# Key pages of mixer A and of its index: turned on the host and loaded page by page from SyncE, instead of gathered by GpSimd and turned on TensorE

## The reference

```python
ki_all = concatenate([cache_a_kidx[page_table].reshape(n, PAST_LEN, D_IDX), ki], axis=1)
sc = where(causal, index_scores(qi, wi, ki_all), -inf)        # sum_h w * relu(q_idx . k_idx)
_, idx = lax.top_k(sc, 256)
k_g, v_g = cache_a_k[phys, off], cache_a_v[phys, off]         # or the new rows
out_a = attend_selected(qa, k_g, v_g, idx <= qpos)            # softmax(q k / 8) v
```

## Time and profile before

| | us |
|---|---|
| median of 3 runs (2168.15 to 2175.05) | 2169.51 |
| the profiled execution, its own time | 2170.43 |
| its span | 2168.6 |
| first part, before the first gather (0 to 444.2) | 444.2 |
| the stretch of `idx` (735.6 to 905.6) | 170.0 |
| the stretch of `sel` up to `a0` (1451.8 to 1501.3) | 49.5 |
| `a0` to `a7` (1501.3 to 1877.7) | 376.4 |

### The profile page before, as it was taken

One profiled execution on the slowest core, in us unless ns is written; L12 is line 12 of the kernel. 1 busy time (PEld: TensorE's weight loads), 2 busy tenths in 40 slices (PEclk: granted clock), 3 DMA queues, 4 the chain that ended last, 5 costly groups with the idle time before them and its releaser, 6 DMA issues.

```text
span 2168.6 us, 27262 instructions
## 1 busy us (share of the span) xinstructions
PE 1698.0 (78%) x8774; PEld 1236.0 (57%) x8774; DVE 1602.5 (74%) x3603; ACT 1257.1 (58%) x2751; POOL 635.5 (29%) x657
## 2 busy tenths in 40 slices
PE   7997699776896985996977987975887796765766
PEld 3554565635664654674655765654655665564554
DVE  2455676486699899869896796886898889768444
ACT  1223434226467654667897697874555465446665
POOL 1000000034334344333333333333333433333431
PEclk9998589886898886997998997987896897876666
DMA  7000300179999999999999999996999999999997
GB/s 277 20 17 13 88 1 30 49 284 420 417 414 390 419 418 390 419 379 384 419 419 374 406 400 371 419 411 248 412 368 362 405 370 385 316 417 358 420 420 302
DMA packets 108351, 695.68 MB, mean 321 GB/s; under 512 B 16688, under 2 KB 19120, under 8 KB 31408
## 3 DMA queue, kind: packets, MB, share of 16 engines
q0 software_dynamic: 95376, 674.29, 77.3%
q1 hardware_dynamic: 12832, 19.65, 3.0%
HBM read 690.14 MB, written 3.76 MB: 320 GB/s over the span
## 4 chain that ended last, share of the span: by engine, by line
PE 33%; DVE 30%; DMA 13%; ACT 10%; DVEq 4%; issue 4%; ACTq 3%; POOL 1%; POOLq 0%
DMA region<-in_peer_rows,region 12%; DVE region L1707 11%; DVE xall L1715 6%; PE ps L2244 5%; PE ps L2049 5%; DVEq L1112 4%; ACTq L1096 3%; ACT region L1100 3%; PE ps L1731 3%; PE ps L1996 2%; PE ps L2066 2%; ACT region L1097 1%; DVE region L1443 1%; PE ps L1899 1%; ACT region L1019 1%
## 5 line engine op out<-in xcount | busy, mean ns | idle before, releaser
L693 POOL DMA_INDIRECT region<-in_peer_rows,region x576 | 569.5, 989 | 1404.1 <-PE ps L2244 712.3
L1707 DVE SCALAR_TENSOR_TENSOR region<-region,h_now 128x1024 f32<-128x1024 f32 x576 | 695.7, 1216 | 208.5 <-DMA region<-in_peer_rows,region 191.8
L2244 PE MATMUL ps<-ident,region 128*128 128x128 f32 x3352 | 567.6, 327 | 253.9 <-ACT region L1100 231.8
L2244 PEld LDWEIGHTS ps<-ident,region 128*128 128x128 f32 x3352 | 472.6, 170 | 358.9 <-ACT region L1100 303.0
L1100 ACT ACTIVATE region<-region 128x1024 f32<-128x1024 f32 x419 | 481.3, 1149 | 35.5 <-issue 1.6
L1095 ACT ACTIVATE region<-region 128x1 f32<-128x1 f32 x576 | 114.5, 199 | 353.1 <-DVE region L1707 348.6
L2049 PE MATMUL ps<-w_uk_s,region 128*128 128x512 f32 x544 | 279.8, 640 | 7.1 <-ACT region L960 6.9
L1715 DVE SCALAR_TENSOR_TENSOR xall<-region,xall 128x1024 f32<-128x1024 f32 x157 | 201.8, 1285 | 68.3 <-ACT region L1097 53.3
L1097 ACT ACTIVATE region<-region 128x1 f32<-128x1 f32 x576 | 169.8, 295 | 40.7 <-issue 1.4
L2049 PEld LDWEIGHTS ps<-w_uk_s,region 128*128 128x128 f32 x544 | 100.2, 205 | 82.6 <-issue 73.9
L960 ACT ACTIVATE region<-ps 128x512 f32<-128x512 f32 x136 | 79.5, 585 | 68.7 <-PE ps L2049 66.0
(11 more groups left out here) (393 smaller groups left out, 2577.3 us busy)
## 6 DMA issues: line engine op xcount, KB each, us to landing
region<-in_w_peer_q POOLq DMA_DIRECT2D x16, 1024.0 KB
region<-in_peer_rows,region POOLq DMA_INDIRECT x576
region<-in_w_in POOLq DMA_DIRECT2D x8, 882.0 KB, 14.1
region<-in_w_peer_q SPq DMA_DIRECT2D x8, 512.0 KB, 4.3
region<-in_x_turned SPq DMA_DIRECT2D x5, 512.0 KB, 3.6
region<-in_w_out SPq DMA_DIRECT2D x2, 1024.0 KB, 12.4
region<-in_w_out SPq DMA_DIRECT2D x1, 2048.0 KB, 18.3
out_p_y<-xall SPq DMA_DIRECT2D x4, 512.0 KB
```

Of the source, the lines that this page charges most:

```text
L693: pool.indirect_dma_start(ring[r][:], None, a["peer_rows"], bass.IndirectOffsetOnAxis(ap=experts[:, t, n:n + 1], axis=0)).then_inc(landed[ ...
L1707: v.scalar_tensor_tensor(ring[r][:, 0:D], ring[r][:, 0:D], 1.0, h_now[:], ALU.mult, ALU.mult, accum_out=acts[:, t % 2, n:n + 1]).then_inc( ...
L2244: last = te.matmul(ps[6 + c // 4][:, (c % 4) * P:(c % 4 + 1) * P], ring[r][:, D + c * P:D + (c + 1) * P], ident[:], is_transpose=True, sta ...
```

## The change

- The host stores the pages of `cache_a_k` and `cache_a_kidx` turned, head dimension first and positions last. This is layout of the inputs and outside the measured time.
- SP loads the pages of keys, values and index keys one by one, 16 for each load of a sample: it reads the page's number from `page_idx` into a register, and issues one DMA of 128 rows of 512 B (64 rows for the index). POOL keeps the pages of mixer B alone. The new keys come as one DMA that turns 8 rows of 128 into 128 partitions of 8 single elements.
- TensorE's transposes of keys and index keys and ScalarE's copies of them are gone; the products read the loaded pages directly. Keys of mixer A are double-buffered, values are not.
- The chains have fewer marks in the same steps: `MA` 24 to 18, `MI` 8 to 5.
- `SHARES`: in steps 100 to 160 DVE adds 1/2 of the rows instead of 2/3, in 362 to 480 2/5 instead of 3/5, 30 rows fewer in all, of which 9 lie in `idx` and 20 in `a0` to `a7`.
- The scores now stand in natural order: ACT's row copies and DVE's write of the mask are plain.

```diff
-        SHARES = [..., (100, 160, 2, 3), ..., (362, 480, 3, 5), (480, 496, 1, 2)]
+        SHARES = [..., (100, 160, 1, 2), ..., (362, 480, 2, 5), (480, 496, 1, 2)]
-        MA, MI, MR, MC, MX = 24, 8, 19, 34, 10
+        MA, MI, MR, MC, MX = 18, 5, 19, 34, 10
...
+            def page_at(g, b):
+                return sp.value_load(page_idx[P // NPG * g:P // NPG * g + 1, b:b + 1], min_val=0, max_val=(NPHYS - 1) * (P // PART))
+            def load_k(b):
+                pages_of = a["cache_a_k"].rearrange("a (s d) k -> (a s) d k", s=P // PART)
+                for g in range(NPG):
+                    sp.dma_start(kT_s[:, b % 2, g, :], pages_of[ds(page_at(g, b), P // PART), :, :].rearrange("s d k -> (s d) k")).then_inc(S[f"k_in{b % 2}"], 16)
+                sp.dma_start(kT_n[:, b % 2, 0:NT], o["s_a_k"][b * NT:(b + 1) * NT, :].rearrange("t d -> d t"), ...).then_inc(S[f"k_in{b % 2}"], 16)
...
+            def index_keys():
+                sp.wait_ge(S["page_idx"], 1)
+                sp.wait_ge(S["dotted"], 70)
+                for b in range(NB):
+                    if b > 1:
+                        sp.wait_ge(S["i_scored"], b - 1)
+                    load_i(b)
+                    for _ in range(MI):
+                        yield
...
             def a_init():
                 hold(sp, S["made"], 4)
-                load_new(k_s, "s_a_k", 0, S["a_new"])
-                load_new(v_s, "s_a_v", 0, S["a_new"])
+                load_k(0)
+                load_v(0)
+                load_k(1)
...
             def mixer_a(b):
                 for j in range(MA):
                     if b + 1 < NB:
-                        if j == 9:
-                            hold(sp, S["k_turned"], 5 * (b + 1))
-                            load_new(k_s, "s_a_k", b + 1, S["a_new"])
-                        if j == 21:
+                        if j == 0 and b:
+                            hold(sp, S["a_scored"], 3 * b)
+                            load_k(b + 1)
+                        if j == 15:
                             hold(sp, S["a_weighted"], b + 1)
-                            load_new(v_s, "s_a_v", b + 1, S["a_new"])
+                            load_v(b + 1)
...
@@ TensorE
             def mixer_a(b):
+                pe.wait_ge(S[f"k_in{b % 2}"], 16 * (NPG + 1) * (b // 2 + 1))
+                pe.wait_ge(S["q_blk"], b + 1)
...
+                for q, (g0, n) in enumerate(group_cols(NPG + 1, 4)):
+                    if g0 == NPG:
+                        pe.wait_ge(S["a_evac"], 3 * b + 1)
+                    for g in range(g0, g0 + n):
+                        keys = kT_s[:, b % 2, g, :] if g < NPG else kT_n[:, b % 2, :]
+                        bank = ps[3] if 8 <= g < NPG else ps[5]
+                        last = te.matmul(bank[:, g % 8 * NTOK:(g % 8 + 1) * NTOK], keys, q_blk[:], start=True, stop=True)
```

167 lines of the change are left out of this document (59 added, 108 removed).

## The result

The changed kernel is slower: a median of 2220.27 us against 2170.05 us in runs of the same session, a ratio of 1.0221 with a 95% interval of 1.0195 to 1.0247. One of its four runs took 3641.74 us; the ratio leaves it out, and the median of the other three is 2219.34. The forecast was 2192. The direction was right and the time lies within the outer range of 2150 to 2260, but the size was not: +50 us where +22 was worked out, and beyond the 2178 to 2215 of the forecast's own case (chance 0.42). By its number alone the result belongs to the rival "SP the bound, from 2215 on" (0.18), whose mechanism the runs don't bear out. The profiled execution took 2219.34 us, its span is 2217.6.

The account below looks back on a forecast made before the run. DMA bytes were taken to bound the index, and a0 to a7 up to 31 us of slack. Index +9, a0 to a7 +8, mixer A's start +7, score rows -2 made +22 on 2170.4: 2192 us, range 2150 to 2260.

Parts of the forecast that it names:

- SP the bound, from 2215 on: Rival: SP's issue time per page cannot feed a sample in its 14 steps; about 2280 us, chance 0.18.
- The floor in bytes: a0 to a7: the bytes alone, 345 us before the change, need about 366 us after it.
- Part 2: Keys, values, index keys: same bytes in 512 B rows at 3.6 us per MB; 4.9 us in index, 19.6 in mixer A.
- 31 us called slack: a0 to a7 before the change: time above the 345 us of bytes, made by engines waiting for each other.
- The steady part of `a0` to `a7`: a0 to a7: bytes of 366 us plus 5% slack, 18 us, make 384 us, or +8.
- The start of mixer A: At a_init: 48 pages ahead of b6's new rows, VectorE stands 17 to 19 us, gathers cover 12; +7 us.
- part 4: SP's own time: 1.0 us a page; SP keeps up except at a_init, where 7 us are lost, bounds 0 and 70.
- part 3: DMA engines alternate packets of two queues, so pages come just in time; 4 us for late index pages, bounds 0 and 20.
- The index: Index stretch: 5 us for smaller packets and 4 us for late pages, together +9.
- The rows of the scores: Between the index and the search: ScalarE's four copies get shorter, 2 us less.
- Engines set the pace: Rival: gaps carry the pages, lighter VectorE and shorter chains bring a0 to a7 to 362; 2156 us, chance 0.25.
- Small packets cost nothing: Rival: 512 B rows go at q0's price, so 25 us fall away; no change, 2172 us, chance 0.15.

Follow-up runs that it names:

- z3_turned_x2: x2_start with the new keys turned once on TensorE instead of by eight loads of single elements; 2203.96 us, ratio 1.0167.
- x2_start: The changed kernel with only a0's keys loaded at a_init, then b6's new rows and the output, a0's values and a1's keys after; 2202.97 us, ratio 1.0152.
- z1_few: The changed kernel with longer page rows, new keys as plain rows, x2_start's order and index pages asked for one sample earlier; 2207.77 us, ratio 1.0173.
- w2_few_static: z1_few with the page numbers as constants on SP instead of register loads; 2200.91 us, ratio 1.0132.
- x1_static: The changed kernel with SP taking page numbers as constants, without register load or register instructions; 2203.56 us, ratio 1.014.
- w1_nopages: x2_start without the page loads behind the first ones, reusing what the buffers hold; 2156.63 us, ratio 0.9922.
- x4_shares: The changed kernel with the shares of before, VectorE adding 30 rows more, TensorE and ScalarE 30 fewer; 2216.88 us, ratio 1.0213.

## Why the prediction was wrong, point by point

**The floor in bytes came out near, in part by luck.** Part 2 took 3.6 us per MB for q1 from the earlier trace rows; the windows show 3.66 and 3.93, so that term held. It gave 366 us of DMA work for `a0` to `a7`; the trace has (0.760 + 0.158) x 404.9 = 372. But it built on 345 us for the kernel before, at the 2.43 us per MB of the earlier trace rows, where that kernel's own shares give (0.948 + 0.008) x 376.4 = 360. Of the 31 us called slack only 17 were time without DMA work, and the work rose by 12 us, not by 21. On the Trainium skill's statement that transfers reach line rate from 512 B up (DMA: Bandwidth & Descriptors, Specifications) the trace does not agree here: 23 to 26 ns for a packet of 512 B or less and 3.66 to 3.93 us per MB, against 2.44 to 2.54 for 8 KB rows. Without the turned loads, whose packets are smaller still, it is 3.39 in `a0` to `a7` (z3_turned_x2).

**The steady part of `a0` to `a7` was put too high.** I took 384 for the eight samples, 8 more than before, and x2_start, which mends only the order of the start, has 388.2. That looks like a hit and is none: its surplus lies in `a0` (59.2 against 46.9). `a1` to `a7` take 327.7 us in the changed kernel and 329.5 before, where the forecast had some 7 more. Pages do come just in time there, and `a4` waits 15.2 us for its values, but this cost nothing net: DMA work rose by 3 us only (0.95 x 329.5 = 313 to 0.965 x 327.7 = 316) and time without it fell from 16 to 12. That a lighter VectorE and shorter chains did this is likely, not shown by itself.

**The start of mixer A failed, and this is the step that decides.** The forecast had +7 for it. `a0` took 30.3 us more than before, of which x2_start gives back 18.0. The mechanism stood in part 4: 48 pages ahead of mixer B's rows, VectorE stands. It was to stand 17 to 19 us and stood 18.1, but this match is luck. SP took 62.1 us, not 48, until `b_ckv` went out (1506.71 to 1568.82), since its pages came at 1.12, 1.59 and 1.14 us; and VectorE came to b6 46 us after the keys were free (1552.7), not 33, since it had lost time at `a0` first.

What failed is the step behind it, the cost of the stalls: "Up to 5 gathers go on meanwhile, 12 us. 7 us are lost." The cover was there. Between the two stalls POOL issued six gathers (1541.9 to 1553.0), and with these and SP's pages the DMA engines worked on for 12 us; then they mostly stood. The stall at b6, in two parts:

```profile
1553.00:1565.00 12.00, 0.00 (x0) 0.00 (x0) 0.00 (x0) 0.00 (x0) 0.92 (x1) 0.50 0.88 338
1565.00:1576.70 11.70, 5.41 (x21) 4.61 (x22) 4.25 (x8) 4.39 (x12) 0.00 (x0) 0.50 0.24 68
```

But 12 us were set against VectorE's stall. What holds GpSimd back is that TensorE frees no slots, and TensorE stood 23.3 us at b6; POOL's longest wait is 22.8 us. That left the DMA engines 10 us of idle time here (0.12 x 12.0 + 0.76 x 11.7) and some 4 before and behind it. And the stall at `a0`'s keys, "TensorE has stood some us at a0", had been given neither a price nor a place in the sum: 15.1 us, which idled the DMA engines for 6 (share 0.74 from 1518.4 to 1541.9). In all they idled for 0.27 x 77.2 = 21 us of `a0`, before not at all (share 1.01). The other 9 us of the 30.3 are work, 0.73 x 77.2 = 56 us against 47: the pages of the start come all at once and cost more per MB than gathers.

That a short stall is covered and a long one not fits z1_few: its wait of 11.7 us in `a0` cost 1.2 us against w2_few_static. The gathers run slower there, which makes the cover last longer. The 12 us themselves are read from this one stall.

**Why SP came late was half the story too.** Part 4 counted SP's instructions, part 3 the alternation of queues, and the start was costed by the first alone. x1_static shows that 16 pages issued in 7.6 us less leave the wait for them as it was, and w2_few_static that only both together end it. The earlier trace rows alone can't tell turns by packet from turns by whole DMA, since gathers and those stores both have nine packets per engine. The index speaks for packets: 96 pages of five passed beside 61 gathers of nine, more than one page per gather.

**The index failed in its sum.** Forecast 5 for packets and 4 for late pages. Late pages stopped TensorE for 37.2 us, more often than forecast, but they cost about 2 us (DMA share 0.99). The packets cost 3.36 MB x (3.93 - 2.44) = 5.0, as forecast. Two things were missing. The gathers beside the pages grew slower, 67.14 MB x (2.54 - 2.44) = 6.7 us; w1_nopages bears it out for this stretch by its 2.45. And 1.1 MB more fall into the stretch (70.71 MB in all against 69.62), 2.7 us. Together 16.4, where 16.0 were measured. The 4.7 us ahead of the index come on top; I had put all eight samples' packets into the one 5. (Other kernels with SP's index pages begin the index at 737.1 to 743.5 us, those without at 734.8 to 736.7, so some of the 4.7 is scatter.)

**The rows of the scores.** 2 us forecast. The stretch from the index to `a0` is 3.6 us shorter, but it scatters by more than that from kernel to kernel, so the term is neither confirmed nor refuted.

**The sum.** Against the forecast `a0` came out 22 us longer, `a1` to `a7` 9 shorter, the index 7 longer, with 5 more ahead of it, 2 less for the way to `a0` and 3 more behind `a7`, which together are the 27 us by which +22 missed +49.

**The rivals.** "Engines set the pace" (2156) fell: the whole comes to that number only when nearly all pages are left out (w1_nopages, 2156.63). "SP is the bound" (2280): pages are 1.12 to 1.94 us apart in mixer A, above its 1.38 in four of fifteen groups, but 1.31 in the mean, below it, and 1.27 in the index (32 issues in 40.3 us), below 1.33. So it didn't decide in the steady stretches: `a1` to `a7` are no longer than before, and x1_static leaves the index at 185.9. On SP's page the Trainium skill gives a register load a floor of about 600 ns (DMA: Bandwidth & Descriptors, Latency and other measured facts); here it took 273 ns by the median, and other steps made up the rest of the 1.12. Without it and its register instructions a page takes (9.58 - 0.34)/15 = 0.62 us (x1_static). "Small packets cost nothing" (2172) fell with the prices above.

**What remains open.** What makes 8 KB packets slower beside 512 B ones in the index and not in `a0` to `a7`, and why the gathers cost 2.81 us per MB beside rows of 2 KB into 32 partitions. Also the last 3.4 us behind `a7`. And what the lighter VectorE and the shorter chains are worth by themselves in the changed kernel: x4_shares undoes only the shares.

## What to carry to other kernels

When a stall is said to be hidden by a ring of loads in flight, set the cover against the engine that frees the slots, not against another that stands beside it, and price every stall: here 12 us of cover hid a stall of 11.7 us almost whole and left about half of one of 23.3. A load moved from one big indirect DMA to many small ones on another queue has three prices, the issuing engine's time, its packets, and what the queue beside it loses; cost each, and cost the first use, where nothing has run ahead, by itself. Look at what small, urgent transfer stands behind the new ones in the same queue: here the place of one 8 KB load cost 17 us, and a new order alone mended it. And when a stretch comes out as forecast, look at its parts: here two errors met in one number.
